# The high and low halves of split weights: two rings of chunks, or one ring with the halves alternating word by word

## What is computed

```python
D_MODEL = 2048
SEQ = 256
D_FF = -(-8 * D_MODEL // (3 * 256)) * 256      # 5632
...
def mixer(h, layer_idx, w_in, ...):
    proj = h @ w_in                             # 256 x 2048 by 2048 x 6152
    ...                                         # mLSTM heads and differential attention heads
    return jnp.concatenate([hm, ha.astype(hm.dtype)], axis=-1) @ w_out

def swiglu(h, w_gate, w_up, w_down):
    return (jax.nn.silu(h @ w_gate) * (h @ w_up)) @ w_down

def reference(x, ...):
    for l in range(DEPTH):                      # DEPTH is 1
        h = rms_norm(x, norm1_w[l])
        x = x + mixer(h, l, w_in[l], ...)
        h = rms_norm(x, norm2_w[l])
        x = x + swiglu(h, w_gate[l], w_up[l], w_down[l])
    return x
```

## Time and profile before

| what | value |
|---|---|
| median of 3 runs | 1105.91 us (1105.87 to 1106.67) |
| the profiled execution, its own time | 1106.12 us |
| its span, first to last instruction | 1104.2 us |
| PE busy | 1096.4 us, 99% |
| DVE busy | 854.6 us, 77% |
| ACT busy | 616.2 us, 56% |
| granted TensorE clock, mean | 1.000 |
| read from HBM | 209.83 MB, 192 GB/s over the span |

### The profile page before, as it was taken

One profiled execution on the slowest core, in us unless ns is written; L12 is line 12 of the kernel. 1 busy time (PEld: TensorE's weight loads), 2 busy tenths in 40 slices (PEclk: granted clock), 3 DMA queues, 4 the chain that ended last, 5 costly groups with the idle time before them and its releaser, 6 DMA issues.

```text
span 1104.2 us, 12990 instructions
## 1 busy us (share of the span) xinstructions
PE 1096.4 (99%) x4951; PEld 907.3 (82%) x4951; DVE 854.6 (77%) x1037; ACT 616.2 (56%) x771; POOL 3.3 (0%) x18
## 2 busy tenths in 40 slices
PE   8999999999999999999999999999999999999998
PEld 7888887888888888888888888888888888888887
DVE  5676546764565666898998999999999889878886
ACT  7566466754544445456555555555665545635552
POOL 1000000000000000000000000000000000000000
PEclk9999999999999999999999999999999999999999
DMA  9745544564466565465664664665665755675662
GB/s 354 274 166 184 174 143 139 173 208 154 142 202 188 177 200 183 154 221 182 200 223 166 215 211 164 212 215 178 196 214 193 235 191 172 198 224 180 196 204 104
DMA packets 59909, 212.77 MB, mean 193 GB/s; under 512 B 6728, under 2 KB 6856, under 8 KB 59848
## 3 DMA queue, kind: packets, MB, share of 16 engines
q1 hardware_dynamic: 59552, 211.84, 58.5%
q10 hardware_dynamic: 296, 0.11, 0.0%
HBM read 209.83 MB, written 2.10 MB: 192 GB/s over the span
## 4 chain that ended last, share of the span: by engine, by line
PE 97%; DMA 1%; DVE 1%; ACT 1%; issue 0%; ACTq 0%
PE acc L480 14%; PE acc L483 14%; PE acc L482 14%; PE acc L704 11%; PE acc L702 11%; PE acc L703 11%; PE aux L703 3%; PE aux L702 3%; PE aux L704 3%; PE aux L483 3%; PE aux L482 3%; PE aux L480 3%; PE aux L494 2%; DMA w_raw<-in_weights 1%; DMA par<-in_params 0%; PE aux L544 0%
## 5 line engine op out<-in xcount | busy, mean ns | idle before, releaser
L1143 DVE TENSOR_TENSOR w_lo<-w_raw,w_hi 128x1024 fp32r<-128x1024 f32 (+1 forms) x477 | 545.8, 1172 | 178.2 <-ACT w_hi L845 176.4
L845 ACT ACTIVATE w_hi<-w_raw 128x1024 fp32r<-128x1024 f32 (+1 forms) x477 | 476.5, 1018 | 318.1 <-PE acc L704 90.1
L702 PE MATMUL acc<-w_lo,act_hi 128*128 128x512 f32 x473 | 185.0, 391 | 0.0
L704 PE MATMUL acc<-w_hi,act_hi 128*128 128x512 f32 x473 | 184.2, 389 | 0.0
L703 PE MATMUL acc<-w_hi,act_lo 128*128 128x512 f32 x473 | 184.0, 389 | 0.0
L480 PE MATMUL acc<-w_lo,act_hi 128*128 128x512 f32 x448 | 178.1, 398 | 2.4 <-DVE w_lo L1143 2.4
L483 PE MATMUL acc<-w_hi,act_hi 128*128 128x512 f32 x448 | 174.7, 390 | 0.0
L482 PE MATMUL acc<-w_hi,act_lo 128*128 128x512 f32 x448 | 174.5, 389 | 0.0
L704 PEld LDWEIGHTS acc<-w_hi,act_hi 128*128 128x128 f32 x473 | 88.8, 188 | 18.6
L703 PEld LDWEIGHTS acc<-w_hi,act_lo 128*128 128x128 f32 x473 | 88.8, 188 | 18.2
L702 PEld LDWEIGHTS acc<-w_lo,act_hi 128*128 128x128 f32 x473 | 88.8, 188 | 18.1
(11 more groups left out here) (275 smaller groups left out, 1274.8 us busy)
## 6 DMA issues: line engine op xcount, KB each, us to landing
w_raw<-in_weights SPq DMA_DIRECT2D x391, 512.0 KB, 4.0
res<-in_x SPq DMA_DIRECT2D x4, 512.0 KB, 11.0
out<-res SPq DMA_DIRECT2D x8, 256.0 KB, 3.3
xt<-in_x_turned SPq DMA_DIRECT2D x3, 512.0 KB, 8.8
xt<-in_x_turned SPq DMA_DIRECT2D x2, 256.0 KB, 3.9
w_raw<-in_weights SPq DMA_DIRECT2D x2, 256.0 KB, 3.8
w_if<-in_gate_w ACTq DMA_DIRECT2D x1, 64.0 KB, 5.5
par<-in_params ACTq DMA_DIRECT2D x1, 47.0 KB, 3.6
```

What stands on the lines that cost most here:

```text
L702: pe.matmul(bank[:], hi, w_lo[:, slot, cols], start=start, stop=False)
L704: return pe.matmul(bank[:], hi, w_hi[:, slot, cols], start=False, stop=stop)
L845: act.activation(w_hi[:, n % SPLIT, cols], w_raw[:, src % RAW, cols], ACT.Copy).then_inc(hi_done, 1)
L1143: dve.tensor_tensor(w_lo[:, n % SPLIT, cols], w_raw[:, src % RAW, cols], w_hi[:, n % SPLIT, cols].bitcast(F32), ALU.subtract).then_inc(lo_ ...
```

## The change

The two rings become one tile, in which each word of the high half is followed by the word of the low half that belongs to it. `w_hi` and `w_lo` become views of this tile with a step of two words. The whole diff:

```diff
@@ -168,8 +168,8 @@
         act_hi = sb("act_hi", [KT, SEQ], F32R)
         act_lo = sb("act_lo", [KT, SEQ], F32R)
         w_raw = sb("w_raw", [RAW, CH])
-        w_hi = sb("w_hi", [SPLIT, CH], F32R)
-        w_lo = sb("w_lo", [SPLIT, CH], F32R)
+        w_parts = sb("w_parts", [SPLIT, CH, 2], F32R)
+        w_hi, w_lo = w_parts[:, :, :, 0], w_parts[:, :, :, 1]
         stage = sb("stage", [TT, NG])
         scaled = sb("scaled", [TT, NG])
         gated = sb("gated", [TT, NG])
```

## The result

| what | before | changed |
|---|---|---|
| median of 4 runs | 1106.1 us (1105.87 to 1106.67) | 2127.25 us (2126.7 to 2127.98) |
| ratio to before, 95% interval | | 1.9228, 1.9201 to 1.9255 |
| span of the profiled execution | 1104.2 us | 2124.9 us |
| mean granted TensorE clock | 1.000 | 1.000 |

First the head of the page of the changed kernel, and its chain by engine; they answer to the earlier trace rows.

What follows compares the result with a forecast made beforehand. PE, busy 1096.4 of 1104.2 us, was taken as the bound through its weight matmuls' distance. The sum was 1106.1 + 976 - 2 = 2080 us; the case's own range 2021 to 2143, the overall range 1103 to 2145.

Steps and rivals of the forecast that it cites:

- PE sets the time, by the distance of 4575 matmuls: Weight matmuls on PE: 4575 at 226.7 ns, 1037 us, nearly the whole span; all added time lies on this path.
- The signs named: Changed profile: weight matmuls 427 to 453 ns apart, gate product 119 ns, DVE's share 41% to 65%, no low-half waits.
- PE's step of two words halves the stream: PE's moving operand: only every second swept word used, stream part doubles, 440 ns a matmul for 226.7; chance 0.53.
- The rival of an unchanged time: PE's moving operand: reads bring in more than two words, for instance four with two used; 1106 us, chance 0.29.
- The reason given, two side-by-side words at a time: PE's reads: supply of two adjacent words at half of PE's clock, so lone words come at half the rate.
- The other picture used for the bound: PE's reads: same 9.5 bytes per ns of swept memory, only every second word used, so the stream part doubles.
- The size of the term: PE's weight matmuls: 213.3 ns more each, fixed 11 ns kept, 4575 x 0.2133 = 976 us more.
- The upper bound, the doubled distance: PE's weight matmuls: whole distance doubles to 453.4 ns, 1037 us more; top of the case's range, 2143 us.
- What comes back at the start: PE's idle 3 us in the first 50 us: about 2 us covered by a slower PE.
- DVE and ACT are covered: Split work on DVE and ACT: 488 and 387 us more at most, hidden behind a slower PE, costing nothing.
- the rival with DVE as the bound: DVE's splits: one extra pass, 1.07 us per full split, PE not slowed; about 1366 us, chance 0.11.
- ACT's 387 us more: ACT's work on the halves: a whole extra pass at 0.83 ns a word, reaching 1003 us, hidden behind PE.

Runs made afterwards that it cites:

- e1_reads: Changed kernel with high and low halves written as two blocks, only PE's moving operand reading with a step of two words (wrong words multiplied): 2126.2 us.
- e2_writes: Changed kernel's tile, ACT and DVE keeping their gaps, but PE reading 512 side-by-side words (a mixture of high and low): 1106.0 us.
- e8_blocks: Changed kernel without alternation: one tile and ring, each slot's 1024 high words side by side, then its 1024 low words: 1106.2 us, ratio 1.0001.
- e4_pairs: Changed kernel with high and low halves alternating two words by two on all engines instead of word by word: 2127.6 us, ratio to before 1.9233.
- e11_half_gap: Changed kernel with each 512-column weight matmul written as two of 256 columns, 9150 in place of 4575: 2138.0 us.
- e5_quads: Changed kernel with high and low halves alternating four words by four (16 bytes each), nothing left out: 1130.0 us.
- e10_quads_off2: PE reads runs of four words as in e5_quads, but starting 8 bytes behind a multiple of 16; ACT and DVE write blocks: 2126.4 us.
- e9_shift1: Blocks as in e8_blocks, but PE's 512-word operand starts one word off the multiple of 16 bytes (wrong columns multiplied): 1136.9 us.
- e12_lo_only: Blocks as in e8_blocks, but the first of each product's three matmuls reads with a step of two words: 1468.6 us.

## Where the prediction was right, and where its reason was not

*PE sets the time, by the distance of 4575 matmuls.* Right; the chain of the changed kernel is all PE, and 4575 x 0.2243 = 1026 us accounts for the 1020.7 to within 5. The signs named came too: 451.5 ns lies within the 427 to 453, the gate product stays at 119, DVE's share is 41%, and no wait of PE for a low half is left.

*PE's step of two words halves the stream.* Right, shown alone by `e1_reads`, with the rest shown to cost nothing by `e2_writes` and `e8_blocks`. The rival of an unchanged time was said to be decided by whether PE can be served with 19 bytes of swept memory per ns. That was the wrong number: runs of four (17.6) and the step of four (17.8) come close to it, and only the first is fast.

*The reason given, two side-by-side words at a time.* Wrong. It would make pairs fast, and `e4_pairs` is as slow as the change. The other picture used for the bound, swept bytes at 9.5 per ns, gives the right value for steps of two and for pairs, but 865 to 900 ns for a step of four, where 461 were measured, and some 440 for runs of four, where it was 233. It is filled lines of 16 bytes that are read at full rate. Both pictures, though wrong, gave the half rate at a step of two words, so that the time came out right was luck in this part: that the row of the kernel before, one word per cycle, "just shows" a supply in pairs did not follow from it, and fits a supply of four as well. The rival's mechanism was the nearer one, a read of four words of which two are used; only that it is not free when two are left out.

*The size of the term.* 213.3 ns a matmul were taken, the fixed 11 ns kept; 224.3 were measured, 1026 us for 976. `e11_half_gap` names the error: next to nothing fixed (2 ns) stands beside a slow stream, and a column takes 0.88 ns rather than 0.833. What the 0.05 ns over two cycles are stays open. The upper bound, the doubled distance (453.4 ns), was the better guide, and 2127 lies within the case's own 2021 to 2143.

*What comes back at the start.* 2 us expected, 1.9 measured (PE idle 3.0 us in the first 50, then 1.2). Over the whole span it is 3.4 us; 0.9 of the rest is one wait of PE for DVE's `a_mat`, which is gone.

*DVE and ACT are covered.* Right, and there was nearly nothing to cover. DVE's feared extra pass of 1.07 us is 1 ns in `e2_writes`, so the rival with DVE as the bound had nothing behind it. The other 3 ns of the changed kernel come with a slower PE, since `e1_reads` has them without any gaps on DVE. ACT's 387 us more were 42.1 (658.3 against 616.2), 39.5 of them in the full splits (488.8 against 449.3); of these `e1_reads`, where ACT writes without gaps, has 9.1, so the larger part is its own writes.

*The rule of the Trainium skill for the rival of no change*, "SBUF — State Buffer", Specifications (TRN2): two hits in a 16-byte line give full bandwidth. For DVE the runs agree (1222 ns a split with two hits a line). For PE's moving operand they don't: two hits a line give 451 ns, and only with all four does it come down to 227 to 243. The size of the line agrees with `e4_pairs`, `e5_quads` and `e10_quads_off2`. *The rule of the Trainium skill for the rival with DVE*, "Vector Engine (DVE) Microarchitecture Reference", section 5.2: full rate only for runs of two adjacent words. The runs differ from it: DVE's step of two words, which its table doesn't hold, takes 1222 ns against 1221 side by side.

## What to carry to other kernels

Lay out what a matmul streams in float32 so that it reads whole lines of 16 bytes: runs of four words or a multiple of that, starting on a multiple of 16 bytes. An interleaving of two data sets in one tile costs DVE nothing (1 ns of 1221, word by word) and ACT up to 87 ns of 1056, but doubles the time of PE when it is by one word or by two; in blocks of 128 words or more it costs nothing. When the trace shows an engine running at its clock with one word a cycle, it says nothing of what a gap costs. Where that engine is 99% busy, measure the pattern on one matmul before choosing a layout. And try the neighbouring patterns too: a step of two could not tell three explanations apart, pairs and runs of four could.

## What the runs showed of the hardware beyond that

- A long run that starts one word off a multiple of 16 bytes costs 6.5 ns a matmul, 31 us in this kernel (`e9_shift1`).
- Interleaving by sixteen words (64 bytes) is slower, 242.6 ns, than by four, 232.7, and by 128, 227.2. The cause stays open.
- ACT's writes have their step at the same place, though a small one: 1143 ns with lone words at PE's old pace, 1129 in the changed kernel, 1128 with pairs and 1057 with runs of four, against 1056 without gaps.
- The loads of the stationary operand last 207 ns in place of 188 beside a slow stream, though their operand is as before. In `e12_lo_only`, with gaps in one matmul of three, it is only the loads of one line of three (L719, 207 ns; L717 and L718, 188).

A row of the loads in the kernel before, then two in the changed one, with idle time that comes from no wait that the profile shows:

```profile
L703 PEld LDWEIGHTS acc<-w_hi,act_lo 128*128 128x128 f32 x473 | 88.8, 188 | 18.2
```

```profile
L704 PEld LDWEIGHTS acc<-w_parts,act_hi 128*128 128x128 f32 x473 | 98.2, 208 | 115.0 <-issue 115.0
L703 PEld LDWEIGHTS acc<-w_parts,act_lo 128*128 128x128 f32 x473 | 98.1, 207 | 112.8 <-issue 112.8
```
